# Two-layer hybrid blocks in fp32: the row norm of the residual by narrow matmuls and a diagonal

## The reference

```python
def rms_norm(x, w):
    x32 = x.astype(jnp.float32)
    y = x32 * lax.rsqrt(jnp.mean(x32 * x32, axis=-1, keepdims=True) + EPS)
    return (y * w.astype(jnp.float32)).astype(x.dtype)
...
    for l in range(DEPTH):
...
        h = rms_norm(x, mix_norm_pre[l]) * (1.0 + sc_m[:, None, :]) + sh_m[:, None, :]
        y = hybrid_mixer(h, positions, w_in[l], q_latent_norm[l], w_q_up[l], w_qidx_up[l],
...
        x = x + g_m[:, None, :] * rms_norm(y, mix_norm_post[l])
        h = rms_norm(x, ffn_norm_pre[l]) * (1.0 + sc_f[:, None, :]) + sh_f[:, None, :]
        y = swiglu(h, w_gate_up[l], w_down[l])
        x = x + g_f[:, None, :] * rms_norm(y, ffn_norm_post[l])
```

## Time and profile before

| | us |
|---|---|
| median of 3 runs | 3350.48 |
| lowest and highest | 3350.16, 3354.29 |
| span of the profiled execution | 3350.1 |
| PE busy | 3136.2 |
| DVE busy | 1578.8 |
| ACT busy | 1274.6 |
| POOL busy | 1297.7 |

### The profile page before, as it was taken

How to read it: one execution, slowest core, us unless ns; L and a number is a source line. 1 busy time by engine, 2 the same in 40 slices (tenths; PEclk the granted TensorE clock), 3 DMA queues, 4 the chain that set the end, 5 groups by cost and what they waited for, 6 DMA issues and landing times. The chain is left out here.

```text
span 3350.1 us, 39423 instructions
## 1 busy us (share of the span) xinstructions
PE 3136.2 (94%) x14764; PEld 2476.2 (74%) x14764; DVE 1578.8 (47%) x2533; ACT 1274.6 (38%) x2494; POOL 1297.7 (39%) x1118
## 2 busy tenths in 40 slices
PE   5998789998999889998999998999989999989998
PEld 3666668886766768886877786888868777768886
DVE  7687366613676354212344643554043455355521
ACT  3335332233335432233354533443234434333432
POOL 2331235543432234443541542444434334424443
PEclk8998799999999889999999998999999999989998
DMA  5322336732421123322321121322223211213222
GB/s 208 121 76 91 118 132 238 246 103 67 123 70 39 38 72 96 100 92 72 123 83 45 45 76 57 101 95 99 93 86 100 70 45 54 92 58 100 95 93 71
DMA packets 92829, 316.50 MB, mean 94 GB/s; under 512 B 12000, under 2 KB 12512, under 8 KB 92512
## 3 DMA queue, kind: packets, MB, share of 16 engines
q1 hardware_dynamic: 92640, 313.99, 28.5%
HBM read 301.36 MB, written 2.10 MB: 91 GB/s over the span
## 5 line engine op out<-in xcount | busy, mean ns | idle before, releaser
L184 POOL TENSOR_TENSOR wl<-raw,wh 128x512 fp32r<-128x512 f32 (+1 forms) x952 | 1238.0, 1304 | 1930.5 <-ACT wh L173 1928.1
L173 ACT ACTIVATE wh<-raw 128x512 fp32r<-128x512 f32 (+1 forms) x952 | 587.4, 623 | 1470.4 <-PE bank L203 1362.3
L201 PE MATMUL bank<-hh,wh 128*128 128x512 f32 x2496 | 1004.1, 402 | 70.9 <-DVE hl L458 46.0
L203 PE MATMUL bank<-hh,wl 128*128 128x512 f32 x2496 | 983.5, 394 | 0.0
L202 PE MATMUL bank<-hl,wh 128*128 128x512 f32 x2496 | 983.5, 394 | 0.0
L201 PEld LDWEIGHTS bank<-hh,wh 128*128 128x128 f32 x2496 | 476.1, 191 | 197.1 <-DVE hl L458 51.8
L203 PEld LDWEIGHTS bank<-hh,wl 128*128 128x128 f32 x2496 | 475.2, 190 | 102.2
L202 PEld LDWEIGHTS bank<-hl,wh 128*128 128x128 f32 x2496 | 476.0, 191 | 95.8 <-issue 0.5
L203 PE MATMUL bank<-hidh,wl 128*128 128x512 f32 x704 | 281.0, 399 | 0.0
L202 PE MATMUL bank<-hidl,wh 128*128 128x512 f32 x704 | 277.5, 394 | 0.0
L201 PE MATMUL bank<-hidh,wh 128*128 128x512 f32 x704 | 276.1, 392 | 0.0
(11 more groups left out here) (361 smaller groups left out, 3899.7 us busy)
## 6 DMA issues: line engine op xcount, KB each, us to landing
raw<-in_w SPq DMA_DIRECT2D x444, 512.0 KB, 3.4
mod_raw2a<-in_wmod SPq DMA_DIRECT2D x28, 512.0 KB, 4.6
mod_raw2b<-in_wmod SPq DMA_DIRECT2D x28, 512.0 KB, 4.5
mod_raw<-in_wmod SPq DMA_DIRECT2D x24, 512.0 KB, 3.7
raw<-in_w SPq DMA_DIRECT2D x32, 384.0 KB, 3.0
first_mods<-in_wmod SPq DMA_DIRECT2D x16, 512.0 KB, 13.9
tmp<-rawb SPq DMA_DIRECT2D x72, 64.0 KB, 2.4
turn<-sine SPq DMA_DIRECT2D x56, 64.0 KB, 2.0
```

Of the source, the lines that this page charges most:

```text
L173: act.activation(self.m.wh[:, t % 2, w_], self.m.raw[:, t % RING, w_], ACT.Copy)\
L184: pool.tensor_tensor(self.m.wl[:, t % 2, w_], self.m.raw[:, t % RING, w_], self.m.wh[:, t % 2, w_].bitcast(F32), ALU.subtract)\
L201: pe.matmul(out, wh, xh, start=start, stop=False)
L203: return pe.matmul(out, wl, xh, start=False, stop=stop)
```

## The change

The sum of squares of x takes the form that the sum of squares of y has. For each tile k PE makes four matmuls with the block of squares as stationary operand and one column of ones as moving one, into columns 4 to 7 of `ps[4]`. ACT's root is on 128x4 (`xroot4`), DVE's reciprocal too (`xinv4`). Then DVE multiplies `ident` with it into `m.acc`, PE multiplies `ones` with `m.acc` into `ps[5]`, and L453 (L463 in the new file) reads `ps[5]` in place of `m.acc`. DVE waits for that matmul at the end of `invert`. Two semaphores are added. In the prelude, `ident` is loaded behind `ones`, and PE's and DVE's first use wait for both.

```diff
@@ tensor(pe) of junction
             if pre:
                 for k in range(KD):
                     pe.wait_ge(square_ready, k + 1)
-                    pe.matmul(ps[4][:], ones, m.sq[:, k % 2, :], start=(k == 0), stop=(k == KD - 1))\
-                      .then_inc(square_used, 1)
+                    for tb in range(NT):
+                        ins = pe.matmul(ps[4][:, NT + tb:NT + tb + 1], m.sq[:, k % 2, tb * P:(tb + 1) * P],
+                                        ones[:, 0:1], start=(k == 0 and tb == 0),
+                                        stop=(k == KD - 1 and tb == NT - 1))
+                    ins.then_inc(square_used, 1)
+                pe.wait_ge(xdiag_ready, 1)
+                pe.matmul(ps[5][:], ones, m.acc[:], start=True, stop=True).then_inc(xinv_ready, 1)
@@ squares(act)
                 act.wait_ge(square_used, KD)
-                act.activation(m.acc[:], ps[4][:], ACT.Sqrt, bias=m.eps[:, 0:1], scale=1.0 / D)\
+                act.activation(xroot4, ps[4][:, NT:2 * NT], ACT.Sqrt, bias=m.eps[:, 0:1], scale=1.0 / D)\
                    .then_inc(xroot_ready, 1)
@@ invert(dve, step)
             dve.wait_ge(xroot_ready, 1)
-            step(dve.reciprocal(m.acc[:], m.acc[:]))
+            step(dve.reciprocal(xinv4, xroot4))
+            dve.tensor_tensor(m.acc[:].rearrange("p (b t) -> p b t", b=NT),
+                              ident.unsqueeze(1).to_broadcast([P, NT, P]),
+                              xinv4.unsqueeze(2).to_broadcast([P, NT, P]), ALU.mult).then_inc(xdiag_ready, 1)
+            dve.wait_ge(xinv_ready, 1)
@@ split(dve, step, scaled)
                     scaled(dve.scalar_tensor_tensor(m.tmp[:, k % 2, :], m.x[:, k, :], pre[0][:, k:k + 1],
-                                                    m.acc[:], ALU.mult, ALU.mult))
+                                                    ps[5][:], ALU.mult, ALU.mult))
@@ prelude
                     sp.dma_start(m.cst[:, C_ONES:C_SEL], a["cst"][:, C_ONES:C_SEL]).then_inc(ones_in, 16)
+                    sp.dma_start(m.cst[:, C_ID:C_ROT], a["cst"][:, C_ID:C_ROT]).then_inc(ones_in, 16)
...
-            for part in (slice(0, C_ONES), slice(C_SEL, C_FREQ)):
+            for part in (slice(C_ROT, C_ONES), slice(C_SEL, C_FREQ)):
...
-            pe.wait_ge(ones_in, 16)
+            pe.wait_ge(ones_in, 32)
...
                 if j == 6:
+                    dve.wait_ge(ones_in, 32)
                     jun.invert(dve, step)
```

More of the change, by code:

```diff
@@ L227, in build @@
     m.mod = fixed("mod", [P, 48 * LAYERS])
-    m.col = fixed("col", [P, 48])
+    m.col = fixed("col", [P, 56])
     m.eps = fixed("eps", [P, 2])
@@ L254, in build @@
     side = m.col[:, 44:45]
+    xroot4, xinv4 = m.col[:, 48:52], m.col[:, 52:56]
     def mod(l, i):
@@ L377, in build @@
     J_SEMS = ("sum_ready", "root_ready", "diag_ready", "inv_ready", "x_ready", "square_ready", "square_used",
-              "xroot_ready", "scaled_ready", "h_head_ready", "h_ready", "order")
+              "xroot_ready", "xdiag_ready", "xinv_ready", "scaled_ready", "h_head_ready", "h_ready", "order")
     def junction(sems, product=None, pre=None, cols=None, start_heads=None, settled=False):
         (sum_ready, root_ready, diag_ready, inv_ready, x_ready, square_ready, square_used,
-         xroot_ready, scaled_ready, head_ready, h_ready, order) = sems
+         xroot_ready, xdiag_ready, xinv_ready, scaled_ready, head_ready, h_ready, order) = sems
         def sync(sp):
```

## The result

| | median us | lowest, highest | runs |
|---|---|---|---|
| before, first chip | 3350.32 | 3349.11, 3354.29 | 4 |
| after, first chip | 3379.27 | 3373.56, 3382.82 | 4 |
| before, other chip | 3355.18 | 3349.98, 3365.43 | 23 |
| after, other chip | 3380.40 | 3374.26, 3387.77 | 6 |
| before, other chip, second set | 3359.55 | 3349.06, 3364.91 | 21 |

The ratio of the kernel after to the kernel before is 1.0071, interval 1.0055 to 1.0088; on the other chip 1.0074, 1.0057 to 1.0091. The kernel is slower by 0.7%, 29 us by the first medians and 25 by the second. 3374.8 was forecast, 24.3 us above before. The profiled execution took 3373.56, with a span 1.8 us shorter. The first four experiments ran with the first set of before on the other chip, the last four with the second set; each ratio and each difference from before is against its own set.

A forecast was written before the change was run, and what follows sets the result against it. PE, busy 94% of the span, was taken to bound the kernel, with losses at stage hand-overs. Terms +23.8 (seven junctions, tail included), +1.6 (prelude) and -1.1 (product starts) gave +24.3 on median 3350.48: 3374.8 us, range 3365 to 3383.

The forecast's parts named there:

- Part 1: From the last sum matmul to the first tmp: 3.49 us in place of 4.22, a gain of 0.73 us each.
- Part 2: Sum of squares of x: narrow matmuls stay at 1.2 GHz, PE paces a 13.8 us loop; with the tail, +23.8 for seven.
- Part 3: Prelude: the longer sum delays DVE's last first_mods reductions and the first tmp by 1.6 us; loading ident costs nothing.
- granted clock 0.50 in all eight junctions: Sign of being right: 1.2 GHz from first narrow piece to first tmp wherever x is normalised before a product.
- Part 4: L453 reading the inverse from PSUM in place of SBUF: nothing either way.
- Part 5: Product starts behind the eight junctions: still at 1.2 GHz at first, for 4.65 us in place of 4.92 each, -1.1 us.
- Rival 1: Sums of x: narrow pieces keep or lift the clock, DVE paces the loop; 3334 us, or about 3341; chance 0.07.
- Rival 2: Sums of x: the clock rises, but late in the loop; about 3343 us, or 3355 at three quarters; chance 0.06.
- Rival 3: Sums of x: semaphore waits at each tile make the loop dearer than its pieces, +1 us each; 3382 us; chance 0.08.
- Rival 4: Whole kernel: nothing moves, because something else hides the places where x is normalised; chance 0.01.

The follow-up runs named there:

- The first four experiments: Changed kernel rerun, 3380.4 us; against it: half the sum matmuls left out, 3351.49; 128 ones columns in x's sum, 3349.22; extra wide matmuls around one-column sums, 3378.3.
- the last four: Changed kernel with 32 columns, 3377.73 us; 128 in both sums plus extra matmuls, 3334.02; kernel before plus extra matmuls, 3348.01; 128 in both sums only, 3343.27.

## Why the prediction was right

Forecast 3374.8, range 3365 to 3383, slower with 0.86; measured 3379.27, and by the difference on the second chip 25.2 against 24.3. By its own steps:

**Part 1, the tail.** 3.49 us forecast, 3.47 to 3.49 measured in all seven. The clock was 0.50 in it, as argued.

**Part 2, the sum.** 13.8 us forecast, 13.81 or 13.82 measured; pieces 0.213 apart; squares waiting on PE. Whole stretch 17.29 forecast, 17.29 measured, +23.8 for seven as forecast. L401 and L406 were the new form in small, which is why the sum is right to a hundredth. The premise that the narrow pieces leave the clock at 1.2 GHz held over 64 in a row, seven times in each of two executions. It was the step with the least behind it, 3.55 us of narrow pieces, and the experiment with 128 columns shows that the whole loss hung on it. The Trainium skill, TensorE: Matmul & The Clock Gate, section on the HAM clock gate, has the clock follow how busy PE was of late; read as time in which matmuls follow one another without a gap, that does not agree with the 13.8 us at 0.50, nor with the clock that fell at 1198.29 while PE never stood.

**Part 3, the prelude.** +1.6 forecast at the reductions. They resume at 37.02, 1.42 later; PE started at 19.76, so the extra DMA cost nothing. The first product matmul is only 1.0 later, since a wait of 0.50 us of DVE between the first tmp and hl is no longer there. The sign "granted clock 0.50 in all eight junctions" holds for seven: in the prelude the column reads 1.00, and only the durations speak for 1.2 GHz.

**Part 4, the PSUM operand.** L463 takes 1.53 us for two, before 1.54: nothing, as forecast.

**Part 5, the product starts.** -1.1 forecast. The starts shortened, 30.56 us at 1.2 GHz for seven, where the earlier trace rows has 39.34 less 5.57, 33.77. At half a microsecond each that is 1.6 us, yet the stretches behind the seven junctions are only 0.2 us shorter in all. The last five behave about as the term says (2.2 us less at 1.2 GHz, 0.8 us shorter); behind the first 0.4 us less gave nothing, and behind the second 0.6 less goes with a stretch 0.6 longer. As a term it was right to about a microsecond; of the 3.1 us that the profile shows beside the junctions, 2.8 come from the first layer's mixer, which the prediction did not treat and which spreads by itself.

**The sum against the median.** I took the profiled execution of before as 0.4 us below the median because its span was. That was wrong: an execution takes 1.8 us more than its span (3373.56 against 3371.8 for the kernel after), and an execution of before on the other chip with the same span of 3350.1 took 3351.88. By that the profiled execution lay some 1.5 us above the first median, not below. The forecast itself, the difference, isn't touched by it. By the profiles the difference is 21.7 us, 2.6 below the forecast, and by the medians 29 and 25; 4.5 us between the forecast and the first median are in no term. Single executions of one kernel spread by over 10 us on one chip. The range was added up from the terms and had no room for that; the junctions were forecast by their mechanism, but that the median fell inside, with 3.7 us to spare, and that 25.2 is so near to 24.3, is in part luck.

**The rivals.** Rival 1 (the narrow pieces lift the clock) did not happen; what it would have been worth is shown by the filled kernel with 128 columns: loop 9.6 and tail 2.53, 1.77 us less a junction where 2.2 had been worked out. The loop did not end 0.5 us earlier: I had let the last eight pieces end 1.0 us behind the last square, but PE has the pieces of two tiles to do from the first of the last two squares on, 2.05 us at 2.4 GHz (the row at 1190.20). A loop of one-column pieces at 2.4 GHz throughout was never run. Rival 2: not once in fourteen junctions. Rival 3: no gap at tile borders. Rival 4: none.

## What to carry to other kernels

A matmul form that is cheaper by its arithmetic may be dearer by the clock: at 1.2 GHz, 32 narrow matmuls cost what eight wide ones did (1.70 against 1.71 us a tile), and they did not raise the clock where the wide ones had. Before a wide operation on the path is swapped for narrow ones, read the granted clock at places of the trace where such narrow ones already run, and price the new form at that clock. Where the narrow form frees something else, here a reciprocal of 3.35 us, widening the moving operand at no cost in weight loads turned a loss of 0.7% into a gain of 0.2%; doing so in both sums and filling PE's waits with matmuls that nobody reads took it to 0.7% below before.

## What the runs showed of the hardware

- The granted clock stayed at 1.2 GHz through 13.8 us of back-to-back matmuls with one moving column, and through the sum with 32 columns (17.34 us with its tail); with 128 columns and the same weight loads it rose 4.37 us into the sum at 1179.55.
- It fell from 2.4 to 1.2 GHz while PE was without a pause, among one-column matmuls with one 128x512 fp32r matmul for every eight pieces (3.41 of 3.41 us busy before the fall at 1198.29).
- A one-column fp32 matmul costs 0.213 us a piece at 1.2 GHz and 0.11 at 2.4 (eight in 0.95 us at 1196.74), with a new weight load each; at 1.2 GHz 32 columns cost the same (17.34 against 17.29 us a junction).
- Two executions of the same program differed by 10.0 us in span with junctions equal to 0.01 us; 6.3 us of it stood in one stretch of the first layer where DVE waits for DMAs of modulation rows (156 GB/s in one, 145 in the other).
